# Gate and up of a feed-forward as 2 by 2 blocks with seven products in place of eight

## What is computed

```python
D_MODEL = 1024
D_FF = 2816
def _layer(...):
    ...
    x = x + _rmsnorm(m @ w_o, g_mq)
    h = _rmsnorm(x, g_fp)
    f = (jax.nn.silu(h @ w_g) * (h @ w_u)) @ w_d
    x = x + _rmsnorm(f, g_fq)
```

## Time and profile before

| | us |
|---|---|
| time, median of 3 runs (1540.48 to 1541.33) | 1540.79 |
| span of the profiled execution, whose own time is not listed apart | 1538.7 |
| first feed-forward matmul, from the span's start | 768.59 |
| one round of the feed-forward (four tiles) | 135.99 |
| end of the last transpose of the output | 1532.8 |
| TensorE busy | 1522.8 |

### The profile page before, as it was taken

How to read it: one execution, slowest core, us unless ns; L and a number is a source line. 1 busy time by engine, 2 the same in 40 slices (tenths; PEclk the granted TensorE clock), 3 DMA queues, 4 the chain that set the end, 5 groups by cost and what they waited for, 6 DMA issues and landing times.

```text
span 1538.7 us, 23001 instructions
## 1 busy us (share of the span) xinstructions
PE 1522.8 (99%) x9877; PEld 1476.1 (96%) x9877; DVE 538.3 (35%) x1003; ACT 490.3 (32%) x936; POOL 141.7 (9%) x177
## 2 busy tenths in 40 slices
PE   7999999999999999999999999999999999999998
PEld 7999999999999999988799999999999999999998
DVE  6104551343114455745642221132122213212335
ACT  6215553452225512346762111111211211111015
POOL 1000000000000034510001001100100100011014
PEclk9999999999999999999999999999999999999999
DMA  5111112111103145144412111111111111111102
GB/s 193 56 41 42 42 43 86 42 29 41 43 28 86 29 137 154 56 137 159 148 50 83 55 42 55 42 43 54 42 55 42 42 55 42 50 47 42 55 28 111
DMA packets 128214, 101.00 MB, mean 66 GB/s; under 512 B 5674, under 2 KB 115250, under 8 KB 128116
## 3 DMA queue, kind: packets, MB, share of 16 engines
q1 hardware_dynamic: 125392, 91.68, 19.4%
q0 software_dynamic: 2720, 7.89, 1.7%
q10 hardware_dynamic: 4, 0.00, 0.0%
HBM read 91.83 MB, written 7.73 MB: 65 GB/s over the span
## 4 chain that ended last, share of the span: by engine, by line
PE 95%; ACT 2%; DVE 2%; issue 1%; DMA 1%; POOL 0%; DVEq 0%; ACTq 0%
PE bank L952 22%; PE bank L501 9%; PE bankC L952 9%; PE bank L503 9%; PE bank L502 9%; PE bank L962 4%; PE bank L960 4%; PE bank L961 4%; PE bankC L501 3%; PE bankC L503 3%; PE bankC L502 3%; PE psT L497 3%; PE bankC L961 1%; PE bankC L960 1%; PE bankC L962 1%; PE psT L708 1%
## 5 line engine op out<-in xcount | busy, mean ns | idle before, releaser
L1631 DVE TENSOR_TENSOR w_lo<-w_raw,w_hi 128x1024 fp32r<-128x1024 f32 x137 | 168.5, 1230 | 441.7 <-ACT w_hi L1548 226.6
L501 PE MATMUL bank<-h_hi,w_hi 128*128 128x344 f32 x752 | 248.6, 331 | 2.7 <-ACT g_pre L1126 2.2
L503 PE MATMUL bank<-h_hi,w_lo 128*128 128x344 f32 x752 | 240.8, 320 | 0.0
L502 PE MATMUL bank<-h_lo,w_hi 128*128 128x344 f32 x752 | 240.5, 320 | 0.0
L952 PE MATMUL bank<-f_hi,w_hi 128*128 128x384 f32 (+1 forms) x696 | 234.4, 337 | 0.0
L952 PE MATMUL bank<-f_hi,w_lo 128*128 128x384 f32 (+1 forms) x696 | 233.8, 336 | 0.0
L952 PE MATMUL bank<-f_lo,w_hi 128*128 128x384 f32 (+1 forms) x696 | 233.7, 336 | 0.0
L501 PEld LDWEIGHTS bank<-h_hi,w_hi 128*128 128x128 f32 x752 | 142.0, 189 | 7.4 <-issue 6.1
L502 PEld LDWEIGHTS bank<-h_lo,w_hi 128*128 128x128 f32 x752 | 141.9, 189 | 0.0
L503 PEld LDWEIGHTS bank<-h_hi,w_lo 128*128 128x128 f32 x752 | 141.8, 189 | 0.0
L2289 POOL TENSOR_TENSOR a_lo<-sg,a_hi 128x384 fp32r<-128x384 f32 (+1 forms) x66 | 61.7, 936 | 774.4 <-ACT a_hi L1459 774.4
(11 more groups left out here) (461 smaller groups left out, 2759.6 us busy)
## 6 DMA issues: line engine op xcount, KB each, us to landing
w_raw<-in_w_in SPq DMA_DIRECT2D x42, 512.0 KB, 3.9
w_raw<-in_w_out SPq DMA_DIRECT2D x24, 512.0 KB, 3.7
w_raw<-in_w_gate SPq DMA_DIRECT2D x23, 512.0 KB, 3.9
w_raw<-in_w_up SPq DMA_DIRECT2D x23, 512.0 KB, 3.9
w_raw<-in_w_down SPq DMA_DIRECT2D x22, 512.0 KB, 3.4
xin<-in_x_prompt SPq DMA_DIRECT2D x8, 512.0 KB, 7.7
xn<-in_x_prompt SPq DMA_DIRECT2D x8, 512.0 KB, 4.7
out_y_prompt<-xn SPq DMA_DIRECT2D x7, 512.0 KB
```

Of the source, the lines that this page charges most:

```text
L501: mm(out[:, 0:TG], w_hi[par][:, ws], hi[:, k, tgc[tg]], start=first, stop=False)
L502: mm(out[:, 0:TG], w_hi[par][:, ws], lo[:, k, tgc[tg]], start=False, stop=False)
L503: return mm(out[:, 0:TG], w_lo[par][:, ws], hi[:, k, tgc[tg]], start=False, stop=last)
L1631: v.tensor_tensor(w_lo[par][:], w_raw[par][:], w_hi[par][:].bitcast(F32), ALU.subtract).then_inc(w_lo_s, 1)
```

## The change

Gate and up of one channel tile, for two quarters of 258 columns, are taken as one product of 2 by 2 blocks. One factor is the two quarters by the two halves of the input channels (four channel tiles each: A11, A12 for the first quarter, A21, A22 for the second), the other the two channel halves of w_gate and w_up. Strassen's form (Winograd's variant) makes the four results from seven block products. The factors are the blocks themselves or sums of them: S1 to S4 from A, made once for each half of the columns, and four sums of weight blocks, made for every pair of gate and up (`t3`, `t2`, and two in place), 128 x 512 each. All sums are in fp32 before the split into high and low.

- **TensorE:** a `pair` is seven `block`s of 4 channel tiles x 3 matmuls of 258 columns, in the order A11, S2, A12, S3, S1, A22, S4, into three banks (0,1,0,1,2,1,2). Four of them add into a bank that another engine has read since. Two sets of three banks take turns. `down` has 16 groups of 12 matmuls (8 output tiles, 2 quarters); the first four are left open for the last tile's low part.
- **Halves:** the two quarters 0 and 1 go through all 22 pairs and the down product, then quarters 2 and 3. Five rounds have four pairs, the sixth has two. So every weight of gate, up and down is loaded and split twice, in pieces of 128 x 512 in six slots (`s_hi`, `s_lo`); TensorE's order fixes the numbering, and slot q is rounded when the block that used it six splits ago is done.
- **ScalarE** (`high`, `pair`): seven roundings of 512, a copy of the first bank (`p1`) between A11 and A12, two silus and two roundings (`a_high`) for a pair.
- **VectorE** (`low`, `pair`): seven low parts of 512, five sums with a bank and two products, 258 columns each. `y_add` after down, 258 columns each.
- **GpSimd:** the four sums for the next pair (`sums_in`, `last_sum`) and the two low parts of the previous pair (`a_low`), except in the last pair of a round, where only the low parts are left; also S1 to S4 (`f_sum`, 1032 columns) and four of the seven low parts of the operands (`f_low`) at the start of each half; the other three are VectorE's.
- **Before the feed-forward:** token tiles are taken in the order 0, 1, 2, 3, 8, 4, 5, 6, 7 (tile 8 holds the eight decoding rows). `HEAD` is gone: the first pair starts when the operands of the first half are ready. The last three tiles are normalised in the first two rounds. x after the mixer is stored to DRAM and read back for the final addition. Ten output tiles are turned in place of nine, since each half has four of the eight decoding rows. Five are turned in the down products of the second half.
- Several semaphores are merged into one; this changes no order.

The core of the diff (`pair` and `down` of an engine are called in turn for both halves and all rounds):

```diff
+STEP = ("A11", "S2", "A12", "S3", "S1", "A22", "S4")
+BANK_OF = (0, 1, 0, 1, 2, 1, 2)
...
+            def pair_load(s, i, j):
...
+                for e, w in enumerate((wg, wu)):
+                    sp.dma_start(w_pair(n)[:, e], chunks(w, 0, 8, 512 * i + P * j, P)).then_inc(raw_in[n % 2], 16)
...
+            def block(s, i, j, o):
+                P_, q, n = pair_no(s, i, j), split_pair(s, i, j) + o, 3 * (j % 2) + BANK_OF[o]
+                out = bank6[n][:, 0:NQ]
+                if STEP[o] in ("A11", "S2", "S1"):
+                    if (s, i, j) == (0, 0, 0):
+                        pe.wait_ge(y_free[0], 7 + n)
+                    elif (s, i, j) == (0, 0, 1):
+                        pe.wait_ge(y_free[1], 9)
+                    elif j < 2:
+                        pe.wait_ge(yd_s, 16 * (ROUNDS * s + i - 1) + (13, 14, 15, 16, 11, 12)[n])
+                    elif BANK_OF[o] == 0:
+                        pe.wait_ge(lu_s, silued(P_ - 2, "g1"))
+                    else:
+                        pe.wait_ge(sum_s, summed(P_ - 2, "C21" if BANK_OF[o] == 1 else "C12"))
+                elif STEP[o] == "A12":
+                    pe.wait_ge(lu_s, silued(P_, "p1"))
+                elif STEP[o] == "S3":
+                    pe.wait_ge(sum_s, summed(P_, "u2"))
+                elif STEP[o] == "A22":
+                    pe.wait_ge(sum_s, summed(P_, "u3"))
+                else:
+                    pe.wait_ge(sum_s, summed(P_, "C22"))
+                if i == 0 and j == 0:
...
+                pe.wait_ge(sp_lo, q + 1)
+                hi, lo = slot(q, 0), slot(q, 1)
+                xh, xl = f_operand(o, 0), f_operand(o, 1)
+                begin = STEP[o] in ("A11", "S2", "S1")
+                for k in range(4):
+                    mm(out, hi[:, k, :], xh[:, k, :], start=(begin and k == 0), stop=False, skip_group_check=True)
+                    mm(out, hi[:, k, :], xl[:, k, :], start=False, stop=False, skip_group_check=True)
+                    ins = mm(out, lo[:, k, :], xh[:, k, :], start=False, stop=(k == 3), skip_group_check=True)
+                ins.then_inc(pe_ev, 1)
+            def down(s, i, aside={}):
+                last, groups, P_, qd = (s, i) == (1, ROUNDS - 1), down_groups(s, i), pair_no(s, i, PAIRS[i] - 1), split_down(s, i)
+                first, kc, base = opened(s, i), PAIRS[i], 16 * (ROUNDS * s + i)
...
+                for d in range(first):
+                    product(d, range(kc - 1))
+                for d in range(first):
+                    product(d, range(kc - 1, kc))
+                for d in range(first, 16):
+                    if d in aside:
+                        aside[d]()
+                    product(d, range(kc))
...
+            def high(q):
+                if q >= SPLITS:
+                    return
+                s, i, o = place_of(q)
+                n = 7 * PAIRS[i]
+                if q >= SLOTS:
+                    act.wait_ge(pe_ev, used_after(q - SLOTS))
...
+                if o < n and o % 7 in (1, 3, 4, 5):
+                    act.wait_ge(tw_s, 4 * pair_no(s, i, o // 7) + {3: 1, 4: 2, 1: 3, 5: 4}[o % 7])
+                else:
+                    load = (load_pair_no(s, i, o // 7) if o < n else
+                            load_down_no(s, i, (o - n) // 4))
+                    act.wait_ge(raw_in[load % 2], 32 * (load // 2 + 1))
+                fn(slot(q, 0), split_source(q), ACT.Copy).then_inc(sp_hi, 1)
...
+            def pair(s, i, j):
+                P_, q, e = pair_no(s, i, j), split_pair(s, i, j), event_pair(s, i, j)
+                turning = (s, i, j) == (0, ROUNDS - 1, 1)
+                high(q + 5)
+                act.wait_ge(pe_ev, e + 1)
+                if P_ >= 2:
+                    act.wait_ge(sum_s, summed(P_ - 2, "prod1"))
+                else:
+                    act.wait_ge(f_t, PLACE[8] + 1)
+                x, y, z = (bank6[3 * (j % 2) + b][:, 0:NQ] for b in range(3))
+                fn(part(P_, "p1"), x, ACT.Copy).then_inc(lu_s, 1)
+                if j:
+                    a_high(P_ - 1, j - 1, 1)
+                    a_high(P_ - 1, j - 1, 0)
+                high(q + 6)
+                high(q + 7)
+                act.wait_ge(pe_ev, e + 3)
+                if P_ >= 2:
+                    act.wait_ge(sum_s, summed(P_ - 2, "prod0"))
+                fn(part(P_, "g1"), x, ACT.Silu).then_inc(lu_s, 1)
+                high(q + 8)
+                high(q + 9)
+                if turning:
+                    f_high(1, F_SPLIT[0])
+                high(q + 10)
+                if turning:
+                    f_high(1, F_SPLIT[1])
+                act.wait_ge(sum_s, summed(P_, "C21"))
+                fn(part(P_, "p1"), part(P_, "p1"), ACT.Silu).then_inc(lu_s, 1)
+                high(q + 11)
...
+            def low(q):
+                if q >= SPLITS:
+                    return
+                dve.wait_ge(sp_hi, q + 1)
+                v.tensor_tensor(slot(q, 1), split_source(q), slot(q, 0).bitcast(F32), ALU.subtract).then_inc(sp_lo, 1)
...
+            def pair(s, i, j):
+                P_, q, e = pair_no(s, i, j), split_pair(s, i, j), event_pair(s, i, j)
+                turning = (s, i, j) == (0, ROUNDS - 1, 1)
+                x, y, z = (bank6[3 * (j % 2) + b][:, 0:NQ] for b in range(3))
+                p1, u2, u3, g1 = (part(P_, x) for x in ("p1", "u2", "u3", "g1"))
+                low(q + 4)
+                low(q + 5)
+                dve.wait_ge(lu_s, silued(P_, "p1"))
+                if P_ >= 2:
+                    dve.wait_ge(al_s, 2 * P_ - 2)
+                dve.wait_ge(pe_ev, e + 2)
+                v.tensor_tensor(u2, y, p1, ALU.add).then_inc(sum_s, 1)
+                low(q + 6)
+                low(q + 7)
+                dve.wait_ge(pe_ev, e + 4)
+                v.tensor_tensor(u3, y, p1, ALU.add).then_inc(sum_s, 1)
+                low(q + 8)
+                dve.wait_ge(pe_ev, e + 5)
+                dve.wait_ge(sum_s, summed(P_, "u3"))
+                v.tensor_tensor(u3, z, u3, ALU.add).then_inc(sum_s, 1)
+                low(q + 9)
+                dve.wait_ge(pe_ev, e + 6)
+                v.tensor_tensor(p1, y, p1, ALU.add).then_inc(sum_s, 1)
+                low(q + 10)
+                dve.wait_ge(lu_s, silued(P_, "g2"))
+                dve.wait_ge(sum_s, summed(P_, "C21"))
+                v.tensor_tensor(u3, u3, p1, ALU.mult).then_inc(sum_s, 1)
+                dve.wait_ge(pe_ev, e + 7)
+                v.tensor_tensor(u2, z, u2, ALU.add).then_inc(sum_s, 1)
+                dve.wait_ge(lu_s, silued(P_, "g1"))
+                dve.wait_ge(sum_s, summed(P_, "C12"))
+                v.tensor_tensor(u2, u2, g1, ALU.mult).then_inc(sum_s, 1)
...
+            def sums_in(s, i, j):
+                P_, n, w = pair_no(s, i, j), load_pair_no(s, i, j), w_pair(load_pair_no(s, i, j))
+                t3, t2 = (tw[:, e, :].rearrange("p (k c) -> p k c", k=4) for e in range(2))
+                pool.wait_ge(raw_in[n % 2], 32 * (n // 2 + 1))
+                if P_:
+                    pool.wait_ge(sp_lo, split_pair(s, i, j - 1) + 4 if j else split_pair(s, i - 1, PAIRS[i - 1] - 1) + 4 if i
+                                 else split_pair(0, ROUNDS - 1, 1) + 4)
+                else:
+                    pool.wait_ge(f_tok, 3)
+                    pool.wait_ge(x1_out[STORED[2]], 16)
+                g_.tensor_tensor(t3, w[:, 1, 4:8], w[:, 1, 0:4], ALU.subtract).then_inc(tw_s, 1)
+                pool.wait_ge(tw_s, 4 * P_ + 1)
+                g_.tensor_tensor(w[:, 1, 0:4], w[:, 1, 0:4], w[:, 0, 0:4], ALU.subtract).then_inc(tw_s, 1)
+                g_.tensor_tensor(t2, t3, w[:, 0, 0:4], ALU.add).then_inc(tw_s, 1)
+            def last_sum(s, i, j):
+                P_, w = pair_no(s, i, j), w_pair(load_pair_no(s, i, j))
+                t2 = tw[:, 1, :].rearrange("p (k c) -> p k c", k=4)
+                pool.wait_ge(tw_s, 4 * P_ + 3)
+                pool.wait_ge(sp_lo, split_pair(s, i, j) + 1)
+                g_.tensor_tensor(w[:, 0, 0:4], w[:, 0, 4:8], t2, ALU.subtract).then_inc(tw_s, 1)
+            def f_sum(s, n):
+                a11, a12 = fb[:, 0:4, quarter(s, 0)], fb[:, 4:8, quarter(s, 0)]
+                a21, a22 = fb[:, 0:4, quarter(s, 1)], fb[:, 4:8, quarter(s, 1)]
+                s1, s2, s3, s4 = (f_source(s, STEP.index(x)) for x in ("S1", "S2", "S3", "S4"))
+                if n == 1:
+                    pool.wait_ge(f_c, 18 if s else 10)
+                    if s:
+                        pool.wait_ge(f_d, 1)
+                        pool.wait_ge(fh_s, 7)
+                        pool.wait_ge(fl_d, DVE_LOWS)
+                    ins = g_.tensor_tensor(s1, a21, a22, ALU.add)
+                else:
+                    pool.wait_ge(sa_s, 4 * s + n - 1)
+                if n == 2:
+                    ins = g_.tensor_tensor(s2, s1, a11, ALU.subtract)
+                elif n == 3:
+                    ins = g_.tensor_tensor(s3, a11, a21, ALU.subtract)
+                elif n == 4:
```

(11 more changed lines are left out.)

1255 lines of the change are left out of this document (683 added, 572 removed).

## The result

The changed kernel takes **1560.0 us** (median of 4 runs, 1557.9 to 1561.2) against 1540.9 before, run beside it: ratio 1.0124, 95% interval 1.011 to 1.0138. It is 1.2% slower; the forecast was 1504. The profiled execution is 1559.3 us long.

What follows compares the result with a forecast made beforehand. TensorE, 99% busy, was taken as the bound: fewer matmuls give -53.5 us, stalls of 20 us in place of 3.2 give back 16.8, so span 1502.0 and time 1504 us; 8 in 10 range 1488 to 1534.

Steps and rivals of the forecast that it cites:

- table loads: Second half: one microsecond more of stalls for table loads (1.28 us each) and the split down groups.
- The gain on TensorE: Feed-forward products: 5808 matmuls at 119.4 ns take 693.5 us in place of 747.9, a gain of 54.4 us.
- VectorE and GpSimd together: Middle pairs: the engines slow each other, making reads late; 0.3 us for each of 20, 6 us, bounds 0 and 46.
- tight read: Inside a pair: a bank read by ScalarE or VectorE between blocks, with about 0.85 us slack before TensorE waits.
- the third: Pairs bound by VectorE and GpSimd in turn, durations adding in full: middle pair 12.3 us, 1553 us, slower; chance 0.10.
- The start: Feed-forward start: waits for operands and second-pair sums in GpSimd's queue, overlapping ScalarE's drains; 7 us, bounds 2 and 12.
- The middle: Between halves: GpSimd's queue outlasts the down product's 11.5 us cover, second pair's sums late; 6 us, bounds 1 and 10.
- The tail: Kernel end: ten tiles turned in place of nine, +0.9 us; behind the last transposes, the same chain on three tiles.
- What would show it: Signs in the later profile: matmuls every 118 to 120 ns, middle pairs 10.0 to 10.5 us, GpSimd releasing early-pair stalls.
- rivals 3 and 2: Pairs bound by VectorE and GpSimd alternately, 1553, chance 0.10; tight reads slip in every pair, 1526 us, or worse streaming, 0.19.

Runs made afterwards that it cites:

- narrow sums: The changed kernel with GpSimd's four weight sums of a pair cut to 2 of each 128 columns, except for the first pair of all: 1513.4 us.
- the one with the scaling moved: The version with sums on VectorE and late f transposes spaced out, plus ScalarE's scaling of the last three tiles moved later: 1515.5 us.
- the fastest version: The version with the middle rearranged (1511.0 us), with the start's four f-operand sums moved to VectorE and GpSimd's last first-pair weight sum earlier: 1507.8 us.

## Why the prediction was wrong

The spans say 1559.3 where the forecast had 1502.0, 57.3 us more. Place by place, by the starts of the blocks, and beside it the kernel with narrow sums (us beyond the time without a stall):

| place | forecast | changed kernel | narrow sums |
|---|---|---|---|
| the length of a matmul, 5808 | 0 | 3.8 | 3.8 |
| feed-forward starts later than 768.6 | in the 7 | 4.9 | 1.8 |
| first round of pairs | 7 | 10.5 | 6.9 |
| second round of pairs | 0 | 7.8 | 1.2 |
| down product of the second round, beyond its 24 transposes | 0 | 5.4 | 3.8 |
| the other ten rounds of pairs | 6 | 33.1 | 0 |
| change of halves | 6 | 8.6 | 7.7 |
| behind the last product | 0 | 3.1 | 3.1 |
| sum (forecast: with 1 for table loads) | 20 | 77.2 | 28.3 |

20 + 57.3 is 77.3, so the table holds all of it. The two columns differ mainly in the rounds of pairs, by 43.4 us, and there by the weight sums. They don't in two other rows: up to the first feed-forward matmul both kernels do the same work, so 4.9 and 1.8 are two executions of one thing, and the 5.4 and 3.8 of the second round's down product have the same waits and differ by the clock after them.

**The gain on TensorE was right.** A round of down products takes 22.99 us as said, 119.7 ns a matmul; in the pairs it is 40.41 / 336 = 120.3 ns, 0.9 over the forecast, 3.8 us in all. The 54 us are there, and the narrow sums show them: 1538.7 less 53.5, less the 3.2 of stalls before, plus the 28.3 of the table is 1510.3, which is the span measured.

**The step that failed is "VectorE and GpSimd together".** Its sign and rows were right and the price was 6 us with bounds of 0 and 46; it cost 43.4 in the rounds of pairs, seven times the price and close to the upper bound. Three things in the step were wrong. It costed the exchange for GpSimd (9.4 us of 10.0 in a middle pair; measured 7.7), which stands in no listed wait of TensorE, and left VectorE at 7.8 us, though the earlier trace rows had VectorE's instruction at 1.07 for 0.50 and GpSimd's at 1.19 for 0.93: the dear side was VectorE, and it went to 11.7. It took the delay of a tight read as one held instruction, up to 1.2 us, where two or three stand in a row ahead of it and each is held anew (4.8 us for 1.8). And it took 0.3 us for each of 20 middle pairs for no row at all, between ends far apart. The row that was nearest, VectorE's 1.07 for 0.50 in the earlier trace rows, put on the seven low parts alone gives 7.8 + 7 x 0.57 = 11.8 us a middle pair, and 11.7 was measured. That it fits so well is partly chance: in the trace some low parts are not held at all, others take up to 1.8 us, and the second product is held too.

**The rival that came true in size** is the third, 1553, at 0.10. Its middle pair of 12.3 us and first pair of 10.8 stand against 11.85 and 10.94. Its mechanism was one exchange of full durations, bound by both engines in turn; what the trace has is VectorE bound (11.7 of 11.85) and GpSimd idle for a third of the pair. I held it unlikely since VectorE's bank reads lie between GpSimd's sums; they do, and run unheld at 0.42, but they are 2.1 us of a pair. That its total is only 7 us off is luck in part: its 55 us hold some 44 for the ten later rounds, which lost 33.1, and losses with other causes fill the gap.

**The start**: 7 us within 2 to 12 for the queue of GpSimd; measured 15.4, and 8.7 with the weight sums narrow from the second pair on. Of the difference 3.6 lie in the first round; the other 3.1 come before any sum is narrow and are no effect of it. The longest waits there are for ScalarE's copy of A11's bank (3.0) and for C22 on VectorE (2.6), not for GpSimd directly. That the same sums would hold the projection's own low parts (3.04 us) and so move the start was not seen: the step asked when GpSimd ends, not whom it holds meanwhile. **The middle**: 6 us, measured 8.6, within its bounds, but by another wait than the one named: not the second pair's sums at the end of GpSimd's queue, but VectorE's y additions behind held low parts, in the down product itself. The number is near by luck. **The second round** and its down product, 13.2 us, had no term at all: the two queues that the first round's x1 and f work fills (ScalarE's scaling ahead of A11's copy, VectorE's copies behind y additions) come from moved code, and the prediction didn't walk through them. **The tail** was called the same chain. Half of its 3.1 us is a wait of 2.1 (0.5 before) for the last y additions, which now stand four in VectorE's queue ahead of the transposes. That was read from the trace and not tried. The other half is the clock after it, granted at 0.50 from 1547.3 to 1550.6: eight transposes take 1.7 us in place of 0.87. The same wait is in all ten traces of kernels with the change, and in five of them the clock stays up. The changed kernel, and the one with the scaling moved:

```profile
1547.32 1.86 PE L714 MATMUL bankC<-ident,yb 128*4 128x128 f32 x8 [2.10 <-DVE yb L2384]
```

```profile
1499.90 1.03 PE L714 MATMUL bankC<-ident,yb 128*4 128x128 f32 x8 [2.10 <-DVE yb L2403]
```

So differences of 1.6 us between single traces say nothing of an edit.

**What would show it** did its work in part: pairs near 12 us with waits for u2 and C22 were named as the signs of rivals 3 and 2, and the low parts' spread (0.67 to 1.85 us) was foreseen. That GpSimd would be the releaser in the first two pairs of each half did not come true: no listed wait of TensorE is for it.

Left open are the rest of the start (u2's wait of 3.7 us in the fastest version), of the change of halves (3.5 us there) and the tail.

## What to carry to other kernels

When a change puts new work on GpSimd beside VectorE, price it as time taken from VectorE: for each VectorE instruction with both inputs in SBUF take its duration beside GpSimd, not alone, add them up for the pair or tile, and only then ask whether that engine still fits under TensorE. If it doesn't, moving the work to the busier engine can be the cure (1560 to 1525 here). An input from PSUM takes the hold away too, but here that was tried only with other numbers in the bank, not as a kernel to keep.
A wait that is tight should have nothing ahead of it in its engine's queue that another engine can hold; and after code has been moved, walk each in-order queue at the seams between phases, where in this case 24 us are lost even with the weight sums narrow, which no steady-state sum shows.

## What the runs showed of the hardware

- The hold is lopsided: a low part of 0.68 us took a median of about 1.7 beside a GpSimd sum, while the sums beside them took a median of 1.61 (1.27 to 2.15) in place of 1.29. With VectorE's second input in PSUM both run at nearly their own speed (0.68 and 1.30 to 1.39).
- After waits of 1.0 and 2.4 us in a TensorE that was busy otherwise the granted clock was 0.73 over 4 us in the changed kernel and 1.00 with narrow sums; the loss was 5.4 and 3.8 us for the same 3.4 us of waits. At the tail a wait of 2.1 us was followed by 0.50 in five of ten traces. Waits of 1.5 us, one in each middle pair, left the clock at 1.00.
- A stall of TensorE is about 0.3 us longer than its listed wait, since the last matmul before it is recorded as 0.28 us long where only 0.12 lie between starts: 3.3 us of waits stand in a round that is 4.3 us longer. VectorE's listed durations likewise overlap by 0.08 us each (0.68 listed, 0.60 to the next start).
- A matmul of 258 columns starts every 119.7 ns in the down product and every 120.3 in the pairs.
